# Expert blocks of a mixture-of-experts step: five instead of four of eight contraction blocks of gate and up as three rounded products

## The reference

```
logits = h @ w_router; scores = sigmoid(logits)
best group of 4 experts, then the top 2 experts in it, weights normalised
gate = h @ w_eg[e]          # 1024 -> 256
up   = h @ w_eu[e]          # 1024 -> 256
a    = silu(gate) * up
y   += combine * (a @ w_ed[e])   # 256 -> 1024
x = x + ga2 * y;  out = rmsnorm(x, final_g)
```

## Time and profile before

| what | value |
|---|---|
| time, median of 3 runs | 1001.68 us (1000.6 to 1001.69) |
| profiled execution, its own time | 1003.87 us |
| span of that execution in the trace | 1002.1 us |
| PE busy | 967.0 us, 96% |
| DVE busy | 711.1 us, 71% |
| ACT busy | 444.7 us, 44% |
| expert blocks | from about 690 us to 972 us |
| final sums and stores | from about 972 us to the end |

### The profile page before, as it was taken

How to read it: one execution, slowest core, us unless ns; L and a number is a source line. 1 busy time by engine, 2 the same in 40 slices (tenths; PEclk the granted TensorE clock), 3 DMA queues, 4 the chain that set the end, 5 groups by cost and what they waited for, 6 DMA issues and landing times.

```text
span 1002.1 us, 17557 instructions
## 1 busy us (share of the span) xinstructions
PE 967.0 (96%) x5660; PEld 775.5 (77%) x5661; DVE 711.1 (71%) x1148; ACT 444.7 (44%) x820; POOL 211.0 (21%) x240
## 2 busy tenths in 40 slices
PE   7899999999999999999989999987999999999996
PEld 4799998999999898799966677665667676766675
DVE  4543988257699953358965665778887878787888
ACT  5442221454222134769862333222555555554634
POOL 3010000000000000314450111001354444534424
PEclk8899999999999999999999999989999999999999
DMA  9954345323434313132265333546778999898757
GB/s 362 359 212 163 106 148 190 108 83 126 160 113 149 128 43 96 43 131 70 70 156 197 127 123 130 189 163 234 262 225 264 320 286 300 298 282 303 190 150 312
DMA packets 66399, 184.70 MB, mean 184 GB/s; under 512 B 9602, under 2 KB 22532, under 8 KB 66332
## 3 DMA queue, kind: packets, MB, share of 16 engines
q1 hardware_dynamic: 57060, 151.02, 43.0%
q0 software_dynamic: 7632, 27.79, 11.2%
q10 hardware_dynamic: 1648, 5.10, 1.3%
HBM read 149.73 MB, written 34.16 MB: 184 GB/s over the span
## 4 chain that ended last, share of the span: by engine, by line
PE 85%; DVE 6%; DMA 4%; ACT 2%; issue 1%; SPq 1%; POOL 0%; ACTq 0%; POOLq 0%; DVEq 0%
PE psum L1492 44%; PE psum L1393 27%; PE psum L1475 5%; PE psum L1766 2%; PE psum L1449 2%; DMA RA<-in_w_ada 1%; DMA RW<-gm_scratch 1%; PE psum L1386 1%; DMA RB<-in_w_exp 1%; DMA RC<-in_w_out 1%; PE psum L1657 1%; PE psum L1607 1%; PE psum L1355 1%; PE psum L1790 1%; DMA RW<-h_scratch,idxc 1%
## 5 line engine op out<-in xcount | busy, mean ns | idle before, releaser
L1393 PEld LDWEIGHTS psum<-input_parts,weight_parts 128*128 128x128 f32 x1824 | 270.4, 189 | 16.3 <-issue 12.8
L1393 PE MATMUL psum<-input_parts,weight_parts 128*128 128x320 f32 x1824 | 277.9, 312 | 3.5 <-DVE input_parts L1922 3.5
L1009 ACT ACTIVATE weight_parts<-RW 128x1024 fp32r<-128x1024 f32 x46 | 48.7, 1058 | 210.7 <-PE psum L1393 166.0
L1492 PE MATMUL psum<-expert_parts,row_of_slot 128*128 128x512 f32 x404 | 133.7, 396 | 0.6 <-ACT row_of_slot L1269 0.6
L1929 DVE TENSOR_TENSOR weight_parts<-RW,weight_parts 128x1024 fp32r<-128x1024 f32 x46 | 56.3, 1225 | 94.2 <-ACT weight_parts L1009 93.8
L1492 PE MATMUL psum<-RB,RW 128*128 x216 | 97.9, 596 | 3.5 <-ACT heads_weight L1265 2.7
L1492 PEld LDWEIGHTS psum<-expert_parts,row_of_slot 128*128 128x128 f32 x404 | 75.6, 188 | 23.6 <-issue 8.0
L818 POOL TENSOR_TENSOR RE<-RE,RA 2x2048 f32<-2x2048 f32 x2 | 9.0, 4514 | 328.3 <-DMA RA<-in_b_ada 328.3
L1277 ACT ACTIVATE expert_parts<-RB 128x2048 fp32r x27 | 51.8, 1917 | 54.2 <-DVEq L2450 20.3
L1492 PEld LDWEIGHTS psum<-RB,RW 128*128 128x128 f32 x216 | 38.9, 190 | 43.6 <-issue 43.3
L1492 PE MATMUL psum<-expert_parts,heads_weight 128*128 128x512 f32 x164 | 67.5, 453 | 0.0
(11 more groups left out here) (410 smaller groups left out, 1744.3 us busy)
## 6 DMA issues: line engine op xcount, KB each, us to landing
RB<-in_w_exp SPq DMA_DIRECT2D x96, 512.0 KB
RW<-in_w_in SPq DMA_DIRECT2D x46, 512.0 KB, 3.4
RW<-in_w_late SPq DMA_DIRECT2D x32, 512.0 KB, 4.5
RA<-in_w_ada SPq DMA_DIRECT2D x10, 512.0 KB, 13.4
RW<-gm_scratch SPq DMA_DIRECT2D x20, 256.0 KB, 3.5
h_scratch<-RE SPq DMA_DIRECT2D x10, 512.0 KB, 2.7
acc_scratch<-RA SPq DMA_DIRECT2D x10, 512.0 KB, 4.0
RB<-acc_scratch SPq DMA_DIRECT2D x10, 512.0 KB, 8.1
```

The lines of the kernel that those rows point to most:

```text
L1009: nc.scalar.activation(spl[:, r, 0], raw[:, r], ACT.Copy).then_inc(whi_ok, 1)
L1393: last = nc.tensor.matmul(psum[:, 2 * r + g, 0:GW], spl[:, r, wv, k], hT[:, xv, k, g * GW:(g + 1) * GW], start=(k == 0 and wv == 0 and xv ...
L1492: return nc.tensor.matmul(out, lhsT, rhs, start=start, stop=stop, **kw_)
```

## The change

Five instead of four of the eight contraction blocks of gate and up are done as three rounded products. The fifth block's weights and tokens get buffers of their own, in a name `more_parts` laid over RE, and in the upper part of `row_of_slot`. `gate_high`, `gate_low` and `x_low` become two operations each, the second of 512 (for `x_low` 128) elements a partition, and the semaphore is raised by the second one. `x_chan` keeps its two operations, with 3 and 5 blocks in place of 4 and 4. The last expert blocks' token numbers can't lie in RE any more: they go to RW, which holds fetched token rows, so SP waits for the last `x_trans` before it issues their load. Three small routing tables move to free columns of `gcol`.

```
-SK = 4
+SK = 5
+SB = 4
+        more_home = [[None, None], [None, row_of_slot[:, 2 * D:2 * D + 2 * FE]]]
+    with nc.sbuf_tensor("more_parts", [P, 3 * T], F32R) as more_parts:
+        for i, (b, v) in enumerate(((0, 0), (0, 1), (1, 0))):
+            more_home[b][v] = more_parts[:, 2 * D + i * 2 * FE:2 * D + (i + 1) * 2 * FE]
+        xTm = more_parts[:, 2 * D + 6 * FE:2 * D + 6 * FE + 2 * P].rearrange("p (b t) -> p b t", b=2)
-    token = RE[:, 2 * D:2 * D + T]
+    token = RW[:, 0:T]
...
         sp.wait_ge(tok_ps, 2)
+        sp.wait_ge(xt_ps, pairs * 2 + 4)
         sp.dma_start(token, a["token"].partition_broadcast(P)).then_inc(tab_in, 16)
...
-            nc.scalar.activation(gate_home[r][0], wexp[:, bass.ds(off, G_U)], ACT.Copy).then_inc(whi_ok, 1)
+            nc.scalar.activation(gate_home[r][0], wexp[:, bass.ds(off, G_U)], ACT.Copy)
+            nc.scalar.activation(more_home[r][0], wexp[:, bass.ds(off + G_U, 2 * FE)], ACT.Copy).then_inc(whi_ok, 1)
...
             for k in range(SK):
-                for xp, v in ((xTh, 0), (xTl, 0), (xTh, 1)):
-                    last = mm(psum[:, r, :], xp[:, r, k], gate_home[r][v][:, k * 2 * FE:(k + 1) * 2 * FE], False,
+                low = xTl[:, r, k] if k < SB else xTm[:, r]
+                for xp, v in ((xTh[:, r, k], 0), (low, 0), (xTh[:, r, k], 1)):
+                    last = mm(psum[:, r, :], xp, gate_home[r][v][:, k * 2 * FE:(k + 1) * 2 * FE] if k < SB else more_home[r][v], False,
                               k == SK - 1 and v == 1)
...
-            nc.vector.tensor_tensor(xTl[:, r].rearrange("p k t -> p (k t)"), psum[:, 4, 0:SK * P],
-                                    xTh[:, r].rearrange("p k t -> p (k t)"), ALU.subtract).then_inc(xl_ok, 1)
+            nc.vector.tensor_tensor(xTl[:, r].rearrange("p k t -> p (k t)"), psum[:, 4, 0:SB * P],
+                                    xTh[:, r, 0:SB].rearrange("p k t -> p (k t)"), ALU.subtract)
+            nc.vector.tensor_tensor(xTm[:, r], psum[:, 5, 0:P], xTh[:, r, SB], ALU.subtract).then_inc(xl_ok, 1)
...
-            nc.vector.tensor_tensor(gate_home[r][1], wexp[:, bass.ds(off, G_U)], gate_home[r][0], ALU.subtract)\
-                .then_inc(wlo_ok, 1)
+            nc.vector.tensor_tensor(gate_home[r][1], wexp[:, bass.ds(off, G_U)], gate_home[r][0], ALU.subtract)
+            nc.vector.tensor_tensor(more_home[r][1], wexp[:, bass.ds(off + G_U, 2 * FE)], more_home[r][0], ALU.subtract).then_inc(wlo_ok, 1)
```

More of the change, by code:

```diff
@@ L84, in program @@
         gate_home[1].append(row_of_slot[:, 0:2 * D])
+        more_home = [[None, None], [None, row_of_slot[:, 2 * D:2 * D + 2 * FE]]]
         xl0 = LATE * T
-        xTl = row_of_slot[:, xl0:xl0 + 2 * SK * P].rearrange("p (b k t) -> p b k t", b=2, k=SK)
-        aTh = row_of_slot[:, xl0 + 2 * SK * P:xl0 + 2 * SK * P + 2 * FE].rearrange("p (b j t) -> p b j t", b=2, j=2)
+        xTl = row_of_slot[:, xl0:xl0 + 2 * SB * P].rearrange("p (b k t) -> p b k t", b=2, k=SB)
+        aTh = row_of_slot[:, xl0 + 2 * SB * P:xl0 + 2 * SB * P + 2 * FE].rearrange("p (b j t) -> p b j t", b=2, j=2)
         heads_lo = row_of_slot[:, 0:2 * D].rearrange("p (k n) -> p k n", k=2)
@@ L277, in program @@
     assert mb + 4 * FE <= 19 * D and 19 * D + 2 * FE <= rb + 2 * D
-    G_U = SK * 2 * FE
+    G_U = SB * 2 * FE
     D_U = KD * 2 * FE
@@ L503, in program @@
     counts, nblk, ends, total = (scratch(NE) for _ in range(4))
-    wsum, eidf, blk0, third = scratch(NT), scratch(NBLK), scratch(NBLK), scratch(NBLK)
+    third = scratch(NBLK)
     BATCH = NT - 3
@@ L523, in program @@
     passed = gfree[:, 4 * N2:4 * N2 + NB2 * (NT - 1)].rearrange("p (n b) -> p n b", b=NT - 1)
+    kept0 = 4 * N2 + NB2 * (NT - 1)
+    eidf, blk0, wsum = gfree[:, kept0:kept0 + NBLK], gfree[:, kept0 + NBLK:kept0 + 2 * NBLK], gfree[:, kept0 + 2 * NBLK:kept0 + 2 * NBLK + NT]
     picked = pairs_a[0][:, 0:2 * BATCH * NE]
```

## The result

The changed kernel takes 1026.45 us (median of 4 runs, 1023.22 to 1028.63) against 1001.14 us for the kernel before (4 runs on the same chip). The ratio is 1.0259, 95% interval 1.0241 to 1.0276: 25.3 us slower. The profiled execution has a span of 1025.1 us, 23.0 more than the 1002.1 of before.

A forecast was written before the change was run, and what follows sets the result against it. TensorE bounds the kernel, VectorE's ring just behind; the change makes that ring the bound. Loop +28.1, blocks 0 and 1 +2.7, behind the last block's start +0.7: 31.5 on 1001.7 gives 1033.2 us, range 1026.5 to 1043.

The forecast's parts named there:

- Two rings: Loop: TensorE's own ring falls from 10.07 to 9.91 us; VectorE's, closed through TensorE, grows from 9.78 to 11.08, the new period.
- four marks: Changed trace: first three-fold load idles for gate_low's second line, period 11.1, VectorE in the loop's chain, slot_owner without idle.
- rival 1: Loop: TensorE stays the bound and gets faster, each block saving 0.16 us, 997.3 us in all; chance 4%.
- hand-over: Loop, VectorE's ring: time from the end of gate_low to the next S, taken as 0.30 us.
- S: Each block: the second load of TensorE's three-fold products, from where the stream is even; start point for measuring the rings.
- ScalarE's late blocks: Loop: slow register loads start gate_high late, holding up gate_low by 0.5 us in 8 of 25 blocks, 4 us.
- VectorE's late starts: Loop: three late starts of gate_low's line by VectorE itself, 1.2 us, stay after the change.
- Blocks 0 and 1: Ahead of the loop: longer x_low wait, products, gate_high and gate_low stand in series, +2.7 us (1.2 to 2.7).
- rival 4: Loop: TensorE's clock falls to 0.83 through pauses of 1.2 us a block, +32 us, 1065 us; chance 3%.
- The token load: End of the blocks: the later load of token numbers for slot_owner is hidden, 0 us; bounds 0 and 6.6.
- second `x_low` operation: Each block on VectorE: 128 elements from PSUM, taken as 0.25 us and hidden in idle time before out_rows.
- the tail: Behind the last S: three more products, +0.69 us.

The follow-up runs named there:

- e1: Changed kernel with its new VectorE and ScalarE operations, but TensorE keeping the four plain and twelve rounded products of before: 1012.09 us, ratio 1.0132.
- e2: Kernel before with only TensorE's part, three plain and fifteen rounded products a block, no new VectorE or ScalarE operation: 1006.02 us, ratio 1.0068.
- e10: Changed kernel with a separate signal for gate_low's first operation; only the fifth contraction block's products wait for the second: 1014.05 us, ratio 1.0152.
- e3: Changed kernel with gate_high ahead of gate_silu on ScalarE and gate_low ahead of out_rows on VectorE: 1008.52 us, ratio 1.0087.
- e6: Changed kernel with e3's two order swaps, and register reads moved to the start of each loop step on three engines: 1009.57 us, ratio 1.0061.
- e7: Changed kernel with VectorE's x_low(0) moved ahead of gate_low(0), before the loop: 1022.05 us, ratio 1.0197.
- e11: Changed kernel with e6's order swaps and early register reads plus e7's exchange of x_low(0) and gate_low(0): 1006.8 us, ratio 1.0107.
- e9: Kernel before with e3's two order swaps and GpSimd's scatters of expert rows replaced by an index-column copy: 996.88 us, ratio 0.9980.
- e12: Kernel before with register reads at the start of each loop step and x_low(0) ahead of gate_low(0): 995.79 us, ratio 0.9968.

## Why the prediction was right, and where its sizes were off

**Two rings, and the change on the one with less room: right.** Three of the four marks that the prediction named are in the trace: the idle time of the first three-fold load ended by `gate_low`'s second line, a period near 11, no idle time of `slot_owner`. The fourth, VectorE in the chain of the loop, isn't, and there the view misleads (see above); the case for the ring rests on the timeline and the experiments. e1, e2 and e10 measured the ring in parts: 10.23 with the operations alone (9.78 + 0.61 = 10.39 by my sum), 10.32 with the products alone (10.47), 10.42 without the shared signal. e3 and e6 show the other ring, 9.90 against the 9.91 forecast. With the orders of e3, rival 1 (TensorE stays the bound) would have had the period right, though not the time.

**The ring's length: 10.95, not 11.08.** The mis-sized term is the hand-over from the end of `gate_low` to S, 0.30 us from rows 5. In the changed kernel it is 798.41 − 798.26 = 0.15, or 0.16 by the unrounded times, and so it is in every block in which TensorE stood idle ahead of S: in the changed kernel, in e1 and e7, in e2 (behind the long operation of 2048 columns) and in block 1 of the kernel before (706.45 + 2.29 = 708.74, S at 708.91, rows 8). The prediction took rows 5 for such a block. TensorE's loads there, in the kernel before, say otherwise:

```profile
839.66 0.19 PEld L1492 LDWEIGHTS psum<-RB,RW 128*128 128x128 f32 x1 [0.24 <-issue]
840.25 0.19 PEld L1492 LDWEIGHTS psum<-expert_parts,heads_weight 128*128 128x128 f32 x1 [0.39 <-DVE expert_parts L2516]
```

Only the load at 840.25 came late. The last plain load stands at 839.66, and two steps of 0.43 us behind it is 840.52, which is S: TensorE's own plain products set it, as in an undisturbed block (the second block is alike, 869.88 + 0.86 = 870.74, its S). So VectorE's ring in the kernel before is 6.00 + 1.20 + 2.28 + 0.16 = 9.64 and has 0.43 us to spare, not 0.29. The sums then come out at 10.25 for e1 (10.23 measured), 10.33 for e2 (10.32) and 10.94 for the change (10.95). In e10 S comes 0.22 to 0.27 behind the end of the first operation, mostly 0.23, which gives 10.40 (10.42); no run shows why it is 0.07 us more there. The forecast was too long by 25 × 0.13 = 3.3 us from this term.

**ScalarE's late blocks: 4.0 us forecast, none measured.** The prediction kept 8 late blocks since nothing in the trace said what makes the reads slow. In the changed kernel `gate_high` starts 1.37 to 1.80 us behind `gate_silu` in all of the loop's blocks, and VectorE waits for it only once there, for 0.15 us. The register reads of `gate_high`:

```profile
L1281 ACTq TENSOR_LOAD <-eidI x27: 273/456/698, 685.1 to 977.9; - x27
L1282 ACTq TENSOR_LOAD <-offI x27: 272/281/295, 685.8 to 978.7; - x27
```

No read is over 698 ns, against 1005 in rows 7. It is the same scatter as before, but with a period of 10.95 us it falls at another place among the reads: none of the 180 reads between 715 and 970 us starts 1.0 to 4.1 us behind a scatter's start, where in the kernel before 44 of 192 start 2.1 to 4.0 us behind it, 24 of them slow. With e1's period of 10.23 us the late blocks are back. This also takes away the 1.2 us that I kept for VectorE's late starts (their idle times add up to 1.0 in the trace). Whether an unexplained delay survives a change can't be read from how often it occurred: it was a coincidence in time between two engines, and the change moved both.

**Blocks 0 and 1: 2.7 us forecast, 3.7 measured, and 1.3 more in block 1 to 2.** The series of waits was as described, but behind the longer pauses the clock fell, which I had weighed only as a rival for the whole loop (rival 4). In the loop, with pauses of some 0.8 us on PE in each block, it stayed at 1.00; the swings between levels that the Trainium skill (TensorE: Matmul & The Clock Gate, "A second HAM failure mode: psum-queue depth-cycling") lets one expect of short pauses didn't come there. The 15 three-fold products from 709.32 took 5.28 us where those from 798.31 took 3.74.

**The sum.** 31.5 forecast, less 3.3 (hand-over), 4.0 and 1.2 (slow reads), plus 1.0 (blocks 0 and 1), 1.3 (block 1 to 2) and 0.7 (24 periods averaging 10.98 in place of 10.95) gives 26.0, against the 26.1 of the table. The misses partly cancel. In the profiled spans −3.1 us of unchanged work ahead of the blocks come on top; the medians, 25.3 apart, don't show these. The token load (0: hidden, 3.9 us long), the second `x_low` operation (0.28 us, hidden; I had 0.25) and the tail (0.5 for 0.7) were right. The total is therefore better than its parts: 8.5 us of misses one way stand against 3.0 the other. The low side of the range had been built from the misses that came, no late blocks and a shorter hand-over.

**Where the change could have gained.** TensorE's saving of 0.16 us a block is real (9.90 in e3, e6 and e11). To collect it takes three moves, and then the gathers, 11.4 us in a full DMA, are the next limit. No version of the changed kernel has a median below that of the kernel before beside it. 0.16 us in 27 blocks, 4.3 us, is less than what the ring took (19.4) and what blocks 0 to 2 took (6.3).

## What to carry to other kernels

Cost an edit on every ring that closes through it, not on the engine it relieves: here 0.16 us off the ring with nothing to spare and 1.30 us onto one that had 0.43 to spare made the period 0.88 us longer. Take a hand-over only from a place where the waiting engine stood idle, and not from one where its own work ended at the same time. Where an operation is split in two, give each part its own signal before counting the second as free. And put register reads ahead of a wait that stands there anyway: in this kernel that alone took 0.3% off, while their delays had looked like scattered noise of single blocks.

## What the runs showed of the hardware that was not expected

- A register read from SBUF takes 0.28 us on ScalarE and 0.30 us on TensorE and VectorE, and up to 1.65 us where it starts 2.1 to 5.4 us behind the start of an indirect scatter's issue on GpSimd, on all three engines. Without the scatters none was over 0.33 us between 715 and 970 us (e9).
- The hand-over from VectorE to an idle TensorE was one number: 0.05 us from the end of the operation to the waiting load and 0.16 to the next load, behind 512 and behind 2048 columns (changed kernel, e1, e2, e7). In e10, behind the first of the two operations, it was 0.12 and 0.23; why is open.
- VectorE's sequencer runs ahead of its engine: in the changed kernel it read the register of the next `down_low` at 796.51 and passed a wait of it at 797.47, while `gate_low` ran from 795.37 to 798.26.
- The granted clock of TensorE fell to 0.57 behind a pause of 2.50 us, to 0.77 behind one of 1.88 and to 0.50 behind one of 3.49; pauses of some 0.8 us in every block of the loop left it at 1.00. The length of the pause doesn't decide alone: in e2 the clock stayed at 1.00 behind one of 1.89 us, and in e12 it fell behind one of 1.37.
- A broadcast load of 640 KB took 3.7 to 3.9 us at the end of the blocks and 12.7 us beside the expert weights. The 3.5 us worked out in the prediction from the Trainium skill (DMA: Bandwidth & Descriptors, "Anatomy of one DMA — SWDGE (gpsimd) path") fit the first case only, and the page gives them for DMAs that GpSimd issues, while SyncE issues this one.
